# Spreading the steps of a pair of attention heads over more turns of the weight loop

## The reference, cut to what matters

```
z = einsum('bhqd,bhkd->bhqk', q, k) * scale         # all three kinds
p = softmax(where(causal, z, -inf)); out = p @ v     # moba; forgetting adds log_f_cum differences to z
later = cumsum(log_keep, reverse) - log_keep         # stick-breaking
w = where(mask, exp(log_beta + later), 0); out = w @ v
```

## Time and profile before

| | us |
|---|---|
| median of three runs | 864.04 |
| the profiled execution's own time | 865.95 |
| its span, first to last instruction | 863.7 |
| TensorE matmuls busy | 821.1 |
| TensorE weight loads busy | 797.5 |
| VectorE busy | 645.4 |
| ScalarE busy | 490.3 |
| GpSimd busy | 21.1 |

### The profile page before, as it was taken

One profiled execution on the slowest core, in us unless ns is written; L12 is line 12 of the kernel. 1 busy time (PEld: TensorE's weight loads), 2 busy tenths in 40 slices (PEclk: granted clock), 3 DMA queues, 4 the chain that ended last, 5 costly groups with the idle time before them and its releaser, 6 DMA issues. The chain is left out here.

```text
span 863.7 us, 16848 instructions
## 1 busy us (share of the span) xinstructions
PE 821.1 (95%) x6824; PEld 797.5 (92%) x6824; DVE 645.4 (75%) x1332; ACT 490.3 (57%) x1015; POOL 21.1 (2%) x53
## 2 busy tenths in 40 slices
PE   5798888999999999999999999899989999999998
PEld 5698887999999999999999999778878999999998
DVE  5666766988888887799888786966755797665551
ACT  6744535766666656755554555755645676555440
POOL 1000000000000000000000000700000000000000
PEclk9999999999999999999999999999999999999999
DMA  9755465666665787489988886533414579665540
GB/s 292 261 182 181 132 203 195 199 197 198 213 219 183 268 291 259 146 290 331 338 297 288 275 255 214 148 123 122 135 53 155 182 226 300 220 195 183 184 147 25
DMA packets 151069, 179.44 MB, mean 208 GB/s; under 512 B 5712, under 2 KB 141136, under 8 KB 150992
## 3 DMA queue, kind: packets, MB, share of 16 engines
q1 hardware_dynamic: 149536, 177.65, 62.6%
q10 hardware_dynamic: 432, 0.68, 0.2%
q0 software_dynamic: 1024, 0.03, 0.1%
HBM read 177.27 MB, written 1.05 MB: 206 GB/s over the span
## 5 line engine op out<-in xcount | busy, mean ns | idle before, releaser
L904 DVE TENSOR_TENSOR wlo<-raw,whi 128x512 fp32r<-128x512 f32 x528 | 342.3, 682 | 69.6 <-ACT whi L666 68.6
L1276 PE MATMUL bank<-A,whi 128*128 128x256 f32 x1280 | 367.6, 287 | 14.6 <-DVE wlo L904 9.0
L666 ACT ACTIVATE whi<-raw 128x512 fp32r<-128x512 f32 x528 | 308.4, 621 | 114.9 <-PE bank L1278 106.8
L1277 PE MATMUL bank<-A,whi 128*128 128x256 f32 x1280 | 359.8, 281 | 0.0
L1278 PE MATMUL bank<-A,wlo 128*128 128x256 f32 x1280 | 359.7, 281 | 0.0
L1276 PEld LDWEIGHTS bank<-A,whi 128*128 128x128 f32 x1280 | 246.0, 192 | 18.5 <-DVE wlo L904 10.2
L1277 PEld LDWEIGHTS bank<-A,whi 128*128 128x128 f32 x1280 | 244.1, 191 | 1.0 <-issue 1.0
L1278 PEld LDWEIGHTS bank<-A,wlo 128*128 128x128 f32 x1280 | 243.7, 190 | 0.0
L1276 PE MATMUL bank<-Hhi,whi 128*128 128x256 f32 x528 | 148.6, 281 | 0.0
L1277 PE MATMUL bank<-Hlo,whi 128*128 128x256 f32 x528 | 148.4, 281 | 0.0
L1278 PE MATMUL bank<-Hhi,wlo 128*128 128x256 f32 x528 | 148.4, 281 | 0.0
(11 more groups left out here) (149 smaller groups left out, 818.3 us busy)
## 6 DMA issues: line engine op xcount, KB each, us to landing
mring<-in_w_mod SPq DMA_DIRECT2D x72, 512.0 KB, 6.0
raw<-in_ffn_w_up SPq DMA_DIRECT2D x22, 1024.0 KB, 5.1
raw<-in_w_gate SPq DMA_DIRECT2D x22, 1024.0 KB, 5.8
raw<-in_w_up SPq DMA_DIRECT2D x22, 1024.0 KB, 5.8
raw<-in_w_down SPq DMA_DIRECT2D x16, 1024.0 KB, 6.1
raw<-in_w_in SPq DMA_DIRECT2D x12, 1024.0 KB, 5.6
raw<-in_moba_w_qkv SPq DMA_DIRECT2D x11, 1024.0 KB, 6.8
raw<-in_ffn_w_down SPq DMA_DIRECT2D x8, 1024.0 KB, 6.4
```

The lines of the kernel that those rows point to most:

```text
L666: act.activation(whi[:, i % SPL, k0:k1, 0:width], raw[:, i % RAW, k0:k1, 0:width], ACT.Copy).then_inc(s_whi, 1)
L904: dve.tensor_tensor(lo, raw[:, i % RAW, k0:k1, 0:width], hi.bitcast(F32), ALU.subtract).then_inc(s_wlo, 1)
L1276: pe.matmul(o, hi, xh, start=kg == 0 and not (j and halved(g)), stop=False)
L1277: pe.matmul(o, hi, xl, start=False, stop=False)
```

## The change

The scaling of a pair moves from age 1 to age 2, the two transposes (or sums) from ages 2 and 3 to ages 3 and 4, and the values from age 5 to age 6. The next pair enters when the last one's age is over 2, so three turns after it, except for the last pair of each sixteen heads, which still enters two turns after. Entries of `pending` get a turn from which they are due. `pend()` runs once at the end of every turn instead of after the fourth k tile. In a turn in which a pair is at age 3 or 4 it puts only "unlock" entries, and while pairs are in flight it puts at most one `vturn` or `qkn` in a turn.

```diff
-LAST_AGE = 5
+LAST_AGE = 6
...
+        turns = [0]
...
-        def pend():
-            while pending:
-                kind, ph, at = pending.pop(0)
+        def pend(free=True, force=False):
+
+            while pending and (force or pending[0][3] <= turns[0]) and (free or pending[0][0] == "unlock"):
+                kind, ph, at, _ = pending.pop(0)
+                free = free and (kind == "unlock" or not flight)
...
-            elif age == 1:
+            elif age == 2:
                 st.put("stsum" if kind == "sb" else "scale", n)
-            elif age in (2, 3):
-                m = n + age - 2
+            elif age in (3, 4):
+                m = n + age - 3
...
-                if h // 2 not in v_ready:
-                    pend()
+                while h // 2 not in v_ready:
+                    pend(force=True)
...
-            if waiting and (not flight or flight[-1][1] > 1):
+            if waiting and (not flight or flight[-1][1] > (1 if len(self.heads) % 16 > 12 else 2)):
                 enter()
             for pair in old:
                 advance(*pair)
+            turns[0] += 1
+            pend(not any(pair[1] in (3, 4) for pair in old))
...
-                    pending.append(("qkn", ph, base))
+                    pending.append(("qkn", ph, base, turns[0] + 2))
                 if base >= 16:
-                    pending.append(("vturn", ph, base))
+                    pending.append(("vturn", ph, base, turns[0] + (1 if base == 22 else 2)))
...
-                if kt == 3:
-                    pend()
...
-                pending.append(("unlock", ph, c0))
+                pending.append(("unlock", ph, c0, turns[0] + 2))
```

## The result

Four runs of the changed kernel gave 849.42 to 854.18 us, a median of 850.86, and four of the kernel before a median of 864.7. The ratio is 0.9857, with a 95% interval of 0.9832 to 0.9883. A second set (label `after_again`) gave 0.9871 [0.9852, 0.989]. The gain is 11 to 14 us. Forecast were 855 us, 9.4 us less, in a range of 847 to 864.

The account below looks back on a forecast made before the run. TensorE was taken to bound the kernel, through its waits and half-clock stretches. Waits of -3.3 us and clock of -6.1 us made -9.4 us, so 855 us in the metric, with a range of 847 to 864.

Parts of the forecast that it names:

- 1. *`vturn`: All eight bank waits of `vturn` go, since the copy it needs is done by then: -5.5 us.
- 2. *The wait of `turn n+1` stays: Second head transpose still waits for ScalarE's copy behind two heads' exponentials, 1.5 us in second and third cluster, 1.2 in sixth: 0.
- Rival B: All bank waits go, those of the head transposes too, and the whole clock loss: 842 us; chance 0.07.
- 3. *VectorE's maxima: Start of VectorE's maxima: 0 for softmax clusters, +0.15 us for the sixth; bounds 0.3 us sooner to 0.7 us later.
- Rival C: VectorE reaches the maxima late in six clusters, its scaling stuck behind a waiting `lo`: some 872 us; chance 0.12.
- 4. *First cluster: First cluster, with two table loads: waits of 1.5 us for scaling and 2.5 us for `turn 1`, for 3.5 before: +0.5 us.
- 5. *Tails: Two clusters ending in `o1` and `o3`: `turn 12` or `turn 28` waits in place of `turn 13` or `turn 29`: 0.
- my signs: Sign of being right: head transposes (L1337) still wait for W in six places, two now the first transpose of the pair.
- 6. *Olo: Ends of `o1` and `o3`: last values come later, so an output matmul waits 1.0 us for Olo, twice: +1.6 us.
- 7. *The clock: Three half-clock stretches of 3.4 us go, 5.1 us, and one of two behind the first cluster, 1.0 us: -6.1 us.
- Rival A: The clock falls to half all the same, so only the 3.3 us of waits are gained: 860.7 us; chance 0.21.

Follow-up runs that it names:

- swap: Changed kernel, but in every turn the older pairs advance before the next pair enters: 852.95 us, ratio 0.9873 to the kernel before.
- swap_soft: Changed kernel with softmax pairs' scaling back at age 1 and, for softmax pairs, older pairs advancing before the next enters: 848.15 us, ratio 0.9829.
- vturn_back: Changed kernel with `vturn` and `qkn` again allowed in the turn of the second head transpose (age 4): 858.07 us, ratio 0.9942.
- before_swap_soft: Kernel before the change, with only the order within a turn changed for softmax pairs (older pair first): 856.46 us, ratio 0.9924.
- best_ccol: `best` with the condition's activation and its two table loads at k tile 0 of slab 2 instead of k tile 6: 844.22 us, ratio 0.9779.
- scale_early: Changed kernel with the scaling of softmax pairs back at age 1, order within a turn unchanged: 850.63 us, ratio 0.9864.
- best: `swap_soft` with the last `vturn` ahead of the last scores of each sixteen heads and the last values at age 5: 845.43 us, ratio 0.979.

## Why the prediction was right

Steps as the prediction numbers them.

1. *`vturn`*: -5.5 us forecast, and all eight waits are gone. Putting it back cost 4.5 us of waits on `vturn`.
2. *The wait of `turn n+1` stays*: it does, in the four clusters named, because ScalarE's order is unchanged. Rival B (all bank waits go) falls. The distance and the bank are the same in the changed kernel, `swap` and `swap_soft`; the waits stay in the first and vanish with the order in the other two. So the order is their cause, and the repeated bubble was not want of room. That rule of the Trainium skill ("Perfetto Trace Analysis", Optimization Strategy) says only "can mean", and here it did not.
3. *VectorE's maxima*: they start 0.50 us behind L1332, at the favourable bound. The wait is 1.28 us for 1.53, in the sixth cluster 1.13 for 1.17, where 0.15 more was forecast. Rival C falls.
4. *First cluster*: 1.36 + 2.09 = 3.45 us of waits, forecast 4.0, before 3.5.
5. *Tails*: the wait moved to the first transpose, 1.1 us each for 1.5 and 1.2. The row names the copy of `vturn` (Vn), where my signs named W in all six places; step 5 itself had the copy of `vturn` in the way.
6. *Olo*: 1.9 us, forecast 2.0 in all (1.6 more than before).
7. *The clock*: -6.1 forecast, 9.5 or 10.9 became 3.4, so -6.1 to -7.5. The sum was right for partly wrong reasons. In the first cluster I kept one stretch, and none came; behind the eviction wait I expected none, and one came in both traces. The argument from "a single wait of 2.9 us had no fall behind it" rested on one execution, and a second execution of the same kernel had the fall. The other premise, that the second wait of a pair brings the fall, didn't hold in three of the four clusters of `vturn_back`. So the size of this term is in part luck.

The waits: -3.3 us forecast, -4.8 in the rest. Steps 3, 4 and 5 came out 0.5 to 0.7 us better each, and the 0.8 us of new waits on L1361 I had put at nothing. That gives -4.3; the last 0.5 us has no row. Rival A (the clock falls all the same) falls for these clusters.

What the prediction lacked is term (a). With it two executions of one kernel differ by up to 6 us, which no step accounts for.

## What to carry to other kernels

A wait on a buffer with one owner at a time says who released it, not why so late: look at what stands ahead of the releasing instruction on its own in-order engine. Here a copy of 0.5 us stood behind 1.6 us of exponentials, and more distance moved only the users for which that queue was already empty. When a wait is taken away by a new order, count the next one behind it: three of my forecasts (`swap`, `swap_soft`, `before_swap_soft`) were too good mainly for that reason. And try the order within a turn before the distance between turns: turning it took one small edit and gave more than half of the gain.

## What the runs showed of the hardware that I had not expected

**Two spacings of the same matmul.** With the clock granted in full, 20 us of the weight loop hold 178 or 179 matmuls in one stretch and 173 in another. This is the same stretch of the first trace of the kernel before, and of its second:

```profile
300.00:320.00 20.00, 20.00 (x173) 20.00 (x172) 17.46 (x32) 10.75 (x19) 0.00 (x0) 1.00 0.83 289
```

```profile
300.00:320.00 20.00, 20.00 (x179) 20.00 (x178) 17.97 (x33) 11.23 (x20) 0.00 (x0) 1.00 0.86 297
```

No engine waits in either. Over the 6312 matmuls of the weight loop the slow spacing adds 10 to 23 us to an execution. The one-column matmul stands at 18 places. At two of them the spacing just before is uneven and tells nothing. At the other 16 it changes, in each of the 12 traces that have this matmul, but for one place in one trace: at 160 us of `best_ccol` it is 0.118 us before and behind. There TensorE waited just ahead of the one-column matmul (there L1279):

```profile
159.95 0.35 PE L1279 MATMUL bank<-meanf 128*128 128x1 f32 x2 [0.28 <-DVE ca L1061]
```

Without that matmul the spacing doesn't change at these places. What the state is, and what sets it at the start, stays open.

**The clock behind equal waits.** It fell behind waits of 1.2 to 1.5 and 0.7 us close together in three of five clusters, in both traces of the kernel before the same ones, and behind one and the same wait of 2.9 to 3.0 us in ten of the 13 traces. With such pairs back in four clusters of `vturn_back` it fell behind one. Behind the first cluster it fell with single waits of 2.5 (`swap`), 2.7 (`scale_early`) and 3.4 us (`before_swap_soft`); after the single waits of 1.1 to 1.9 us in the clusters of `before_swap_soft`, `swap_soft` and `best` it never did. So longer waits cost a stretch of 3.4 us more often, but which ones do could not be told from their length here.
